# A depthwise convolution shared by four engines: 22 of 31 taps of two channel tiles as ScalarE products and GpSimd adds

## The chip, the cores and the metric

One core of a Trainium2 chip runs the kernel. The time is device microseconds of one execution, lower is better; the median of the runs is compared. The engines are TensorE (PE; PEld is its weight load), VectorE (DVE), ScalarE (ACT), GpSimd (POOL) and SyncE (SP), which issues the DMAs of the weights here.

## The reference, cut to what matters

Two layers of a transformer on 2 x 128 tokens (128 context tokens and 128 latents), width 1024: first attention with a short convolution and a dense SwiGLU, then a Conformer convolution and a mixture of 8 experts. The change lies in the Conformer convolution, a depthwise convolution of 31 taps over the tokens of each of the two sequences, of 1024 channels:

```python
def _conformer_conv(h, p):
    z = h @ p["w_pw1"] + p["b_pw1"]
    a, g = jnp.split(z, 2, axis=-1)
    u = a * jax.nn.sigmoid(g)
    u = lax.conv_general_dilated(
        u, p["w_dw"][:, None, :], window_strides=(1,),
        padding=((CONF_KERNEL // 2, CONF_KERNEL // 2),),
        dimension_numbers=('NWC', 'WIO', 'NWC'),
        feature_group_count=u.shape[-1]) + p["b_dw"]
    u = jax.nn.silu(_layernorm(u, p["ln_g"], p["ln_b"]))
    return u @ p["w_pw2"] + p["b_pw2"]
```

Everything is float32.

## The kernel before

Activations stand transposed, channels on the partitions: hid, xT and uT have 8 tiles (KT) of 128 channels by 256 tokens (two blocks of 128; uT has 15 columns of zeros on both sides of each block). Weights come in pieces of 1 MB into a ring of 7 slots (raw), in the order of ORDER; ACT rounds each into high, DVE subtracts (low), and PE multiplies in three passes. The ada pieces, the conditioning, are used by PE straight from raw (ada_piece).

Each engine has its own hand-written program; they meet at semaphores. In the convolution stage the order is this. PE computes pw1 in four units of two channel tiles; ACT makes the sigmoid (glu_gate), DVE the product into uT (glu, line 1230). As soon as tiles 0 and 1 are there, DVE begins their taps between its low parts, and it goes on with tiles 2, 3 and 4 in turn: one scalar_tensor_tensor a tap, hid = uT shifted x tap + hid (conv_taps, lines 1236 to 1248; the first tap adds the bias). It waits each time for its own tap of the same tile before. Between them stand rows_out(4), which copies PE's sums of the conditioning out of PSUM into ada4 (line 934), and mod_out(4) (line 945), which adds a bias to them. Tiles 5, 6 and 7 (DVE_TILES = 5 and up) are multiplied by PE: ACT scales the identity by the 128 taps of a tile (diag, line 714, a ring of DIAGS = 6), and PE multiplies uT by it and accumulates in PSUM (line 1835). ACT takes each finished tile out with its bias (conv_out, line 700). PE does ada_sum(4) after the first of its tiles, and one ada_piece of group 5 after each further 6 taps. ada_sum(4) waits for rows_out(4), and the first piece of group 5 for mod_out(4).

When all eight tiles are done, PE adds them over the channels with a matrix of ones (ln_sums, line 1842), DVE subtracts the mean (line 1276), ACT squares (line 722), PE sums again (line 1537), POOL takes the root, and pw2 follows, then the routing and the experts. The sums wait for DVE's tiles by conv_part and for PE's by conv_pe_ready.

POOL has little to do: the roots (line 437), the DMAs of the gate's bias, pw2_gb (line 455, waits for ada_out), and the bias added to xT (line 458, 128x2048).

## Time and profile before

| | us |
|---|---|
| Median of 3 runs | 1578.24 (1577.27 to 1578.58) |
| The profiled execution | 1578.13, of which span 1576.3 |
| PE busy | 1504.0 (95%) |
| PE weight loads busy | 1263.9 (80%) |
| DVE busy | 1194.9 (76%) |
| ACT busy | 969.1 (61%) |
| POOL busy | 22.7 (1%) |

The page gives one execution, taken by the hardware profiler. Engine times are the union of their instructions; PE's ends are modelled, and matmuls overlap. A float32 matmul stands as two records of each kind, so 93 taps are 186 records. In a timeline a row merges instructions of one line: its first number is the start of the first, its second the time to the end of the last. Instructions of DVE and ACT overlap a little, so that the distance between two is less than one's duration.

### The profile page before, as it was taken

How to read it: one execution, taken by the hardware profiler on the slowest of the kernel's cores; microseconds unless marked ns; L12 is line 12 of the kernel's file. 1: busy time of each engine (PE TensorE's matmuls, PEld its weight loads, DVE VectorE, ACT ScalarE, POOL GpSimd, SP SyncE). 2: the span in 40 equal slices, each digit the busy share in tenths (PEclk: the TensorE clock that was granted, in tenths of full speed). 3: DMA queues.
4: the chain of work that ended last, by engine and by line, in shares of the span. 5: the costliest groups of instructions: out<-in, count | busy, mean ns of one | idle time of the engine just before them, and what ended most of it. 6: DMA issues, size and time to landing. Idle time of an engine off the chain costs nothing.

```text
span 1576.3 us, 22550 instructions
## 1 busy us (share of the span) xinstructions
PE 1504.0 (95%) x8346; PEld 1263.9 (80%) x8346; DVE 1194.9 (76%) x1195; ACT 969.1 (61%) x989; POOL 22.7 (1%) x28
## 2 busy tenths in 40 slices
PE   5979989999999879999999999999999999999997
PEld 2858789998887768888888888888888888888885
DVE  2547564444798568889879889888988997988996
ACT  2436253432547357777776777777777777776773
POOL 0110000000000000000000000000000000000000
PEclk9989999999999879999999999999999999999999
DMA  9654586665744429989989998998998998998993
GB/s 364 253 218 176 176 299 222 226 202 192 263 161 161 161 84 373 374 338 355 372 340 357 374 363 330 371 378 323 370 374 323 372 373 323 370 375 322 372 374 132
DMA packets 100877, 468.56 MB, mean 297 GB/s; under 512 B 8108, under 2 KB 38972, under 8 KB 51664
## 3 DMA queue, kind: packets, MB, share of 16 engines
q1 hardware_dynamic: 99408, 464.81, 78.4%
q10 hardware_dynamic: 864, 1.76, 0.3%
q0 software_dynamic: 544, 1.15, 0.2%
q8 instruction: 41, 0.67, 0.2%
q14 instruction: 20, 0.16, 0.0%
HBM read 466.55 MB, written 1.14 MB: 297 GB/s over the span
## 4 chain that ended last, share of the span: by engine, by line
PE 90%; DVE 4%; DMA 2%; ACT 2%; issue 1%; POOL 0%; SPq 0%; ACTq 0%; DVEq 0%
PE bank L1507 20%; PE bank L1505 20%; PE bank L1506 20%; PE bank L1511 6%; PE bank L1512 5%; PE bank L1513 5%; PE bank L1522 2%; PE bank L1935 2%; DMA raw<-ada_w 2%; PE bank L1835 2%; PE bank L1963 2%; PE bank L1790 1%; PE bank L1791 1%; PE bank L1792 1%; DVE hid L1248 1%; PE bank L1537 1%
## 5 line engine op out<-in xcount | busy, mean ns | idle before, releaser
L1401 DVE TENSOR_TENSOR low<-raw,high 128x2048 fp32r<-128x2048 f32 x333 | 748.5, 2289 | 118.3 <-ACT high L784 113.6
L784 ACT ACTIVATE high<-raw 128x2048 fp32r<-128x2048 f32 x333 | 626.6, 1920 | 75.3 <-DMA raw<-moe 70.6
L1505 PE MATMUL bank<-high,hidH 128*128 128x512 f32 x896 | 350.9, 392 | 3.1 <-ACT hidL L774 3.1
L1507 PE MATMUL bank<-high,hidL 128*128 128x512 f32 x896 | 349.9, 391 | 0.0
L1506 PE MATMUL bank<-low,hidH 128*128 128x512 f32 x896 | 349.5, 390 | 0.0
L1511 PE MATMUL bank<-hidH,high 128*128 128x256 f32 x736 | 213.4, 290 | 16.3 <-DVE hidL L912 5.1
L1512 PE MATMUL bank<-hidL,high 128*128 128x256 f32 x736 | 210.9, 287 | 0.0
L1513 PE MATMUL bank<-hidH,low 128*128 128x256 f32 x736 | 210.7, 286 | 0.0
L1505 PEld LDWEIGHTS bank<-high,hidH 128*128 128x128 f32 x896 | 168.7, 188 | 38.0 <-ACT hidL L774 3.5
L1507 PEld LDWEIGHTS bank<-high,hidL 128*128 128x128 f32 x896 | 168.6, 188 | 35.2
L1506 PEld LDWEIGHTS bank<-low,hidH 128*128 128x128 f32 x896 | 168.7, 188 | 34.7
L1505 PE MATMUL bank<-high,upH 128*128 128x512 f32 (+1 forms) x462 | 189.8, 411 | 2.4 <-DVE low L858 2.4
L858 DVE TENSOR_TENSOR low<-raw,high 128x2048 fp32r<-128x2048 f32 (+2 forms) x59 | 132.8, 2262 | 74.4 <-ACT high L490 74.2
L1507 PE MATMUL bank<-high,upL 128*128 128x512 f32 (+1 forms) x462 | 181.9, 394 | 0.0
L1506 PE MATMUL bank<-low,upH 128*128 128x512 f32 (+1 forms) x462 | 181.3, 393 | 0.0
L1511 PEld LDWEIGHTS bank<-hidH,high 128*128 128x128 f32 x736 | 144.1, 196 | 28.4 <-issue 17.3
L490 ACT ACTIVATE high<-raw 128x2048 fp32r<-128x2048 f32 (+2 forms) x59 | 110.8, 1887 | 73.0 <-DMA raw<-ffn_gu 48.2
L788 ACT ACTIVATE eact<-bank 128x256 f32<-128x256 f32 x112 | 43.2, 386 | 170.4 <-PE bank L1507 170.4
L1512 PEld LDWEIGHTS bank<-hidL,high 128*128 128x128 f32 x736 | 144.1, 196 | 0.0
L1513 PEld LDWEIGHTS bank<-hidH,low 128*128 128x128 f32 x736 | 144.0, 196 | 0.0
L1507 PEld LDWEIGHTS bank<-high,upL 128*128 128x128 f32 x462 | 87.4, 189 | 18.4
L1505 PEld LDWEIGHTS bank<-high,upH 128*128 128x128 f32 x462 | 87.6, 190 | 17.7 <-issue 3.2
(225 smaller groups left out, 1381.2 us busy)
## 6 DMA issues: line engine op xcount, KB each, us to landing
raw<-moe SPq DMA_DIRECT2D x336, 1024.0 KB, 4.8
raw<-ada_w SPq DMA_DIRECT2D x48, 1024.0 KB, 6.1
raw<-ffn_gu SPq DMA_DIRECT2D x44, 512.0 KB, 5.0
raw<-ffn_down SPq DMA_DIRECT2D x11, 1024.0 KB, 7.1
raw<-w_in SPq DMA_DIRECT2D x8, 1024.0 KB, 10.2
raw<-conv_pw SPq DMA_DIRECT2D x16, 512.0 KB, 5.2
raw<-w_o SPq DMA_DIRECT2D x4, 1024.0 KB, 6.2
raw<-conv_pw SPq DMA_DIRECT2D x4, 1024.0 KB, 5.3
```

Source lines behind the costliest of these rows:

```text
L490: a.activation(high[:, n % SPLITS, 0:w], raw[:, m % RAWS, 0:w], ACT.Copy).then_inc(S("high_ready"), 1)
L784: a.activation(high[:, m % SPLITS, :], raw[:, n % RAWS, :], ACT.Copy).then_inc(S("high_ready"), 1)
L788: a.activation(eact[:, u % 2, :], bank[:, u % 2, 0:UNIT], ACT.Silu).then_inc(S("e_silu"), 1)
L858: v.tensor_tensor(low[:, STREAM[SPLIT[n]] % RAWS, 0:w], raw[:, STREAM[SPLIT[n]] % RAWS, 0:w], high[:, n % SPLITS, 0:w].bitcast(F32), ALU.s ...
L1401: v.tensor_tensor(low[:, n % RAWS, :], raw[:, n % RAWS, :], high[:, m % SPLITS, :].bitcast(F32), ALU.subtract).then_inc(S("low_ready"), 1)
L1505: pe.matmul(out, xh, wh, start=start, stop=False)
L1506: pe.matmul(out, xh, wl, start=False, stop=False)
L1507: return pe.matmul(out, xl, wh, start=False, stop=stop)
L1511: pe.matmul(out, wh, hidH[:, kk, :], start=start, stop=False)
L1512: pe.matmul(out, wh, hidL[:, kk, :], start=False, stop=False)
L1513: return pe.matmul(out, wl, hidH[:, kk, :], start=False, stop=stop)
L1522: last = pe.matmul(bank[32 * c:32 * c + 32, 6, :], cond[:, k, :], raw[:, m % RAWS, c * 512:(c + 1) * 512], start=k == 0, stop=k == KT - 1)
```

## The change

- The taps are divided anew. DVE does tiles 0 to 3 whole and taps 0 to 8 of tile 4. PE does taps 0 to 8 of tile 5 and tiles 6 and 7 whole (PE_TAPS, 71). Taps 9 to 30 of tiles 4 and 5 (PRODUCTS, 44) are multiplied by ACT, each into a slot of prod (a ring of PRODS = 4), the first two straight into pool_part.
- POOL adds each further product to pool_part, its half for the tile, 42 adds of 128x256. From the third add on it waits for its own add two before.
- DVE joins: hid[4] += pool_part[0], and hid[5] = PE's part from bank 2 + bias + pool_part[1]. The sums of the layernorm wait for this.
- The ring of diagonals has 12 slots instead of 6. ACT makes 12 ahead of glu_gate(2) and 12 products ahead of glu_gate(3), then two diagonals and a product in turn.
- rows_out(4) stands after 5 taps of tiles 2 to 4 instead of 8, mod_out(4) after 9 instead of 11. PE does ada_sum(4) after 30 of its taps, and the pieces of group 5 after 36, 42 and so on.
- POOL does its adds before pw2_gb and the bias of xT.

```diff
--- before.py
+++ after.py
@@ -41,7 +41,8 @@
 Z0 = Q_LORA + KV_LORA + ROPE
 RAWS = 7
 SPLITS = 6
-DIAGS = 6
+DIAGS = 12
+PRODS = 4
 PIECE = 2048
 GROUP = 2048
 GC = GROUP // 512
@@ -64,7 +65,11 @@
 NPAR = _c
 
 
-DVE_TILES = 5
+DVE_TILES = 4
+SHARED = 9
+POOL_TILES = (4, 5)
+PRODUCTS = [(k, j) for j in range(SHARED, TAPS) for k in POOL_TILES]
+PE_TAPS = [(5, j) for j in range(SHARED)] + [(k, j) for k in (6, 7) for j in range(TAPS)]
 PHASE = 12480
 NORM_C, LAT_C, HEAD_C = 8, 10, 16
 HSS_C = HEAD_C + 5 * HEADS
@@ -213,6 +218,8 @@
         sg = sb("sg", [P, UC, TILES, P], where=ph)
         sq = sb("sq", [P, KT, TOK], where=ph)
         diag = sb("diag", [P, DIAGS, P], where=ph)
+        prod = sb("prod", [P, PRODS, TOK], where=ph)
+        pool_part = sb("pool_part", [P, len(POOL_TILES), TOK], where=ph)
         ph.close()
         sb("phase_space", [P, PHASE])
         const = sb("const", [P, C_END])
@@ -450,6 +457,13 @@
                 src = t["ada_b"][1:2, 5 * D + half * 512:5 * D + (half + 1) * 512]
                 for tt in range(TILES):
                     pool.dma_start(gate_b[p0 + tt:p0 + tt + 1, :], src).then_inc(S("gate_bias"), 16)
+            for i in range(2, len(PRODUCTS)):
+                half = PRODUCTS[i][0] - POOL_TILES[0]
+                pool.wait_ge(S("product_ready"), i + 1)
+                if i >= 4:
+                    pool.wait_ge(S("product_added"), i - 3)
+                st.mark(pool.tensor_tensor(pool_part[:, half, :], pool_part[:, half, :], prod[:, i % PRODS, :], ALU.add),
+                        "product_added")
             b0 = COLS["pw2_b"][0]
             pool.wait_ge(S("ada_out"), 10)
             st.do(pool.tensor_tensor(pw2_gb[:, :, :], mod[:, 1, 2], par[:, b0:b0 + KT].unsqueeze(2).to_broadcast(
@@ -695,28 +709,52 @@
                                          ACT.Sigmoid, bias=par[:, b:b + 1]), "sg_ready")
 
             def conv_out(k):
-                a.wait_ge(S("tap_used"), (k - DVE_TILES + 1) * TAPS)
+                a.wait_ge(S("tap_used"), PE_TAPS.index((k, TAPS - 1)) + 1)
                 b = COLS["dw_b"][0] + k
                 st.mark(a.activation(hid[:, k, :], bank[:, 4 + k % 2, 0:TOK], ACT.Identity,
                                      bias=par[:, b:b + 1]), "conv_pe_ready")
+
+            def diagonals(i0, i1):
+
+                for i in range(i0, min(i1, len(PE_TAPS))):
+                    k, j = PE_TAPS[i]
+                    if i >= DIAGS:
+                        a.wait_ge(S("tap_used"), i - DIAGS + 1)
+                    st.mark(a.activation(diag[:, i % DIAGS, :], ident, ACT.Copy,
+                                         scale=taps[:, j * KT + k:j * KT + k + 1]), "diag_ready")
+
+            def products(i0, i1):
+
+                if i0 == 0:
+                    a.wait_ge(S("state_out"), 32)
+                for i in range(i0, min(i1, len(PRODUCTS))):
+                    k, j = PRODUCTS[i]
+                    a.wait_ge(S("glu_ready"), k + 1)
+                    half = k - POOL_TILES[0]
+                    if i >= PRODS + 2:
+                        a.wait_ge(S("product_added"), i - PRODS - 1)
+                    dst = pool_part[:, half, :] if i < 2 else prod[:, i % PRODS, :]
+                    st.mark(a.activation(dst.rearrange("p (t n) -> p t n", t=TILES), uT[:, k, :, j:j + P], ACT.Copy,
+                                         scale=taps[:, j * KT + k:j * KT + k + 1]), "product_ready")
 
             for u in range(4):
                 if u < 3:
                     named("pw1", "a", u + 1)
                     named("pw1", "b", u + 1)
+                if u == 2:
+                    diagonals(0, DIAGS)
+                if u == 3:
+                    products(0, 12)
                 glu_gate(u)
 
-            for k in range(DVE_TILES, KT):
-                for j in range(TAPS):
-                    i = (k - DVE_TILES) * TAPS + j
-                    if i >= DIAGS:
-                        a.wait_ge(S("tap_used"), i - DIAGS + 1)
-                    st.mark(a.activation(diag[:, i % DIAGS, :], ident, ACT.Copy,
-                                         scale=taps[:, j * KT + k:j * KT + k + 1]), "diag_ready")
-                if k > DVE_TILES:
-                    conv_out(k - 1)
-                    named("pw2", 0, k - DVE_TILES - 1)
-            conv_out(KT - 1)
+            for n in range(len(PRODUCTS) - 12):
+                diagonals(DIAGS + 2 * n, DIAGS + 2 * n + 2)
+                products(12 + n, 13 + n)
+                if n == 16:
+                    named("pw2", 0, 0)
+            conv_out(6)
+            named("pw2", 0, 1)
+            conv_out(7)
             for k in range(KT):
                 a.wait_ge(S("centred"), k + 1)
                 st.mark(a.activation(sq[:, k, :], hid[:, k, :], ACT.Square), "ln_sq")
@@ -1261,14 +1299,21 @@
             conv_taps((0, 1), 16, 26)
             glu(3)
             conv_taps((0, 1), 26, TAPS)
-            rest = tuple(range(2, DVE_TILES))
-            conv_taps(rest, 0, 8)
+            conv_taps((2, 3, 4), 0, 5)
             rows_out(4)
-            conv_taps(rest, 8, 11)
+            conv_taps((2, 3, 4), 5, SHARED)
             mod_out(4)
-            conv_taps(rest, 11, 25)
+            conv_taps((2, 3), SHARED, 23)
             named("pw2", 0, 0)
-            conv_taps(rest, 25, TAPS)
+            conv_taps((2, 3), 23, TAPS)
+            v.wait_ge(S("conv_part"), st.n["conv_part"])
+            v.wait_ge(S("product_added"), len(PRODUCTS) - 3)
+            st.mark(v.tensor_tensor(hid[:, 4, :], hid[:, 4, :], pool_part[:, 0, :], ALU.add), "conv_part")
+            v.wait_ge(S("product_added"), len(PRODUCTS) - 2)
+            v.wait_ge(S("tap_used"), SHARED)
+            b = COLS["dw_b"][0] + 5
+            st.mark(v.scalar_tensor_tensor(hid[:, 5, :], bank[:, 2, 0:TOK], par[:, b:b + 1], pool_part[:, 1, :], ALU.add,
+                                           ALU.add), "conv_part")
             named("pw2", 0, 1)
 
             v.wait_ge(S("ln_sum"), 1)
@@ -1823,17 +1868,16 @@
                 if u:
                     ada_piece(4, 4 + u)
 
-            def conv_taps(k, j0, j1):
-
-                if j0 == 0:
-                    pe.wait_ge(S("glu_ready"), k + 1)
-                    if k >= DVE_TILES + 2:
-                        pe.wait_ge(S("conv_pe_ready"), k - DVE_TILES - 1)
-                for j in range(j0, j1):
-                    i = (k - DVE_TILES) * TAPS + j
+            def conv_taps(i0, i1):
+
+                for i in range(i0, i1):
+                    k, j = PE_TAPS[i]
+                    if i == 0 or PE_TAPS[i - 1][0] != k:
+                        pe.wait_ge(S("glu_ready"), k + 1)
                     pe.wait_ge(S("diag_ready"), i + 1)
-                    st.mark(pe.matmul(bank[:, 4 + k % 2, 0:TOK].rearrange("p (t n) -> p t n", t=TILES),
-                                      diag[:, i % DIAGS, :], uT[:, k, :, j:j + P], start=j == 0, stop=j == TAPS - 1),
+                    last = SHARED - 1 if k == 5 else TAPS - 1
+                    st.mark(pe.matmul(bank[:, 2 if k == 5 else 4 + k % 2, 0:TOK].rearrange("p (t n) -> p t n", t=TILES),
+                                      diag[:, i % DIAGS, :], uT[:, k, :, j:j + P], start=j == 0, stop=j == last),
                             "tap_used")
 
             def ln_sums(ks, first, last):
@@ -1843,17 +1887,16 @@
                                     stop=last and k == ks[-1])
                 return ins
 
-            cuts = [(k, j) for k in range(DVE_TILES, KT) for j in range(0, TAPS, 6)]
-            for i, (k, j) in enumerate(cuts):
-                conv_taps(k, j, min(j + 6, TAPS))
-                if i == 5:
+            for n, i in enumerate(range(0, len(PE_TAPS), 6)):
+                conv_taps(i, min(i + 6, len(PE_TAPS)))
+                if n == 4:
                     ada_sum(4)
-                if i >= 6 and i < 12:
-                    ada_piece(5, i - 6)
-            pe.wait_ge(S("conv_part"), DVE_TILES * TAPS)
-            ln_sums(tuple(range(DVE_TILES)), True, False)
-            pe.wait_ge(S("conv_pe_ready"), KT - DVE_TILES)
-            st.mark(ln_sums(tuple(range(DVE_TILES, KT)), False, True), "ln_sum")
+                if n >= 5 and n < 11:
+                    ada_piece(5, n - 5)
+            pe.wait_ge(S("conv_part"), DVE_TILES * TAPS + SHARED + 2)
+            ln_sums(tuple(range(6)), True, False)
+            pe.wait_ge(S("conv_pe_ready"), 2)
+            st.mark(ln_sums((6, 7), False, True), "ln_sum")
             ada_piece(5, 6)
             ada_piece(5, 7)
             for k in range(KT):
```

## Rows read from the trace of the kernel before

**Rows 1.** The page: shares of the chain that ended last, and a group of VectorE.

```profile
PE 90%; DVE 4%; DMA 2%; ACT 2%; issue 1%; POOL 0%; SPq 0%; ACTq 0%; DVEq 0%
...
L1401 DVE TENSOR_TENSOR low<-raw,high 128x2048 fp32r<-128x2048 f32 x333 | 748.5, 2289 | 118.3 <-ACT high L784 113.6
```

**Rows 2.** Busy us (and instructions) of each engine by windows: convolution, experts.

```profile
core 0: us, PE busy (x) PEld busy (x) DVE busy (x) ACT busy (x) POOL busy (x), PEclk, DMA share, GB/s
...
453.00:503.00 50.00, 48.79 (x243) 36.53 (x244) 47.81 (x109) 39.53 (x97) 4.22 (x2) 1.00 0.47 167
...
590.00:1560.00 970.00, 970.00 (x4501) 803.15 (x4500) 850.90 (x635) 707.80 (x609) 0.00 (x0) 1.00 0.92 354
```

**Rows 3.** Timeline, start and end of the convolution: start us, us, engine, line, operation, count.

```profile
453.17 7.16 PE L1835 MATMUL bank<-uT,diag 128*128 128x256 f32 x32 [0.31 <-ACT diag L714]
...
488.41 1.06 PE L1522 MATMUL bank<-raw,cond 128*32 128x512 f32 x8
...
489.40 13.68 PE L1835 MATMUL bank<-uT,diag 128*128 128x256 f32 x62
...
493.70 7.21 DVE L1248 SCALAR_TENSOR_TENSOR hid<-uT,par,hid 128x256 f32<-128x256 f32 x18
...
502.92 3.62 PE L1842 MATMUL bank<-hid,const 128*128 128x256 f32 x16
```

**Rows 4.** Timeline of ScalarE: sigmoids, a weight piece, unhindered diagonals, squares.

```profile
426.50 0.84 ACT L694 ACTIVATE sg<-bank,par 128x256 f32<-128x256 f32 x2 [3.07 <-PE bank L1513]
...
485.39 1.90 ACT L490 ACTIVATE high<-raw 128x2048 fp32r<-128x2048 f32 x1
487.19 1.85 ACT L714 ACTIVATE diag<-const,par 128x128 f32<-128x128 f32 x6
...
507.04 2.73 ACT L722 ACTIVATE sq<-hid 128x256 f32<-128x256 f32 x8 [3.44 <-DVE hid L1276]
```

**Rows 5.** Timeline of GpSimd, 471 to 477 us.

```profile
471.56 0.51 POOL L455 TENSOR_TENSOR pw_gb<-mod,par 128x16 f32<-128x16 f32 x1 [70.93 <-DVE mod L945]
472.15 3.71 POOL L458 TENSOR_TENSOR xT<-xT,pw_gb 128x2048 f32<-128x2048 f32 x1
```

**Rows 6.** VectorE's taps: the tile uT (ns min/median/max), then its timeline.

```profile
engine op xcount: duration ns min/median/max, first and last start us, forms
...
L1248 DVE SCALAR_TENSOR_TENSOR hid<-uT,par,hid x150: 475/480/3834, 421.4 to 500.4; 128x256 f32<-128x256 f32 x150
...
471.51 0.88 DVE L1248 SCALAR_TENSOR_TENSOR hid<-uT,par,hid 128x256 f32<-128x256 f32 x2
...
471.92 4.23 DVE L1248 SCALAR_TENSOR_TENSOR hid<-uT,par,hid 128x256 f32<-128x256 f32 x2
...
476.07 2.06 DVE L1248 SCALAR_TENSOR_TENSOR hid<-uT,par,hid 128x256 f32<-128x256 f32 x5
```

**Rows 7.** Timeline of VectorE ahead of the last GLU gate.

```profile
441.75 8.01 DVE L1248 SCALAR_TENSOR_TENSOR hid<-uT,par,hid 128x256 f32<-128x256 f32 x20
452.77 0.88 DVE L1230 SCALAR_TENSOR_TENSOR uT<-bank,par,sg 128x256 f32<-128x256 f32 x2 [3.01 <-ACT sg L694]
```

**Rows 8.** Granted clock by windows, and TensorE's thin matmuls by timeline.

```profile
562.00:566.00 4.00, 2.09 (x18) 1.85 (x18) 2.54 (x10) 1.85 (x2) 0.00 (x0) 0.99 0.00 0
566.00:570.00 4.00, 2.88 (x14) 2.91 (x14) 3.59 (x4) 0.96 (x3) 0.00 (x0) 0.50 0.02 4
...
503.00:510.00 7.00, 7.00 (x48) 4.87 (x47) 5.04 (x9) 3.53 (x11) 0.00 (x0) 1.00 0.00 0
512.00:518.00 6.00, 3.32 (x13) 2.95 (x13) 3.85 (x9) 2.74 (x6) 0.71 (x1) 0.50 0.00 0
...
508.32 4.27 PE L1537 MATMUL bank<-const,sq 128*128 128x2 f32 x32
...
545.02 3.13 PE L1537 MATMUL bank<-const,hid 128*128 128x2 f32 x16 [1.98 <-ACT hid L501]
```


## Prediction

> **What bounds the kernel now.** The page comes first: the chain that ended last is TensorE for 90% of the span [rows 1]. The stages follow from the busy table by windows. From 590 us to the end, the stage of the experts, PE is busy for all of its 970 us at full clock [rows 2]: whatever reaches that stage late or early moves the end by as much. DMA share is 0.92 there, but it starts its loads on the releases of the same chain, so it moves along. The stage that changes is the convolution, 453 to 503 us, where PE, DVE and ACT are busy 48.8, 47.8 and 39.5 of 50 us and POOL 4.2 [rows 2]. The timelines show what ends it. DVE starts its last 18 taps at 493.70 and is done at 500.91; PE's last 31 taps end at 503.08, and its sums of the tiles for the layernorm (L1842) start at 502.92 [rows 3]. So PE ends the stage now, and DVE is only 2.0 us behind the point at which it would. Taking taps off both at once is a sensible aim; the question is what GpSimd does to DVE.
>
> **The change part by part.** The code has 8 x 31 = 248 taps. Before, DVE does 155 and PE 93. After, DVE does 4 x 31 + 9 = 133, PE 9 + 62 = 71, and 44 are products on ACT: two go straight into the partial sums, 42 are adds on POOL.
>
> PE: 62 records are 31 taps in 13.68 us [rows 3], (13.68 - 0.38)/31 = 0.43 us a tap. 22 fewer are 9.5 us less.
>
> DVE: 18 taps take 7.21 us [rows 3]; with one duration of 0.48 taken off, the other 17 follow at 0.396 us. 22 fewer are 8.7 us less. The two joins cost one pitch each, 0.8 us more.
>
> ACT: it makes 22 diagonals fewer and 44 products more. Diagonals that need not wait for PE come 6 in 1.85 us [rows 4], 0.29 us apart. A product of 128x256 has no row; the squares, 8 in 2.73 us, give 0.33 and the sigmoids, 2 in 0.84, give 0.37 [rows 4]. The product reads two strided halves of SBUF and scales by a column; I take 0.36. An iteration of the new loop (two diagonals, one product) is then 2 x 0.29 + 0.36 = 0.94 us against 0.86 for PE's two taps, and PE has six pieces of the conditioning between (1.0 us each [rows 3]). 32 iterations and one weight piece (1.90 [rows 4]) are 32 us, within the 50 of the stage, so ACT is hidden. If that cover went, each 0.1 us on a product would cost at most 3.2 us.
>
> POOL: an add of 128x256 has no row. The two ordinary TENSOR_TENSORs of this engine in the trace took 0.51 us for 16 elements a partition and 3.71 for 2048 [rows 5]: 1.57 ns an element over 0.49 us, so 0.89 us by my estimate for 256. 42 of them are 37 us, and ACT delivers a product only each 0.95 to 1.3 us. POOL has that time.
>
> But POOL does not run beside DVE for nothing. While POOL adds the bias to xT (472.15 to 475.86), one DVE tap takes 3.83 us against a median of 0.48. It is the second of the two that start at 471.92 and end 4.23 us later, so it starts at 472.31, and the next starts at 476.07 [rows 5, 6]. That is 476.07 - 472.31 - 0.40 = 3.36 us lost in a POOL instruction of 3.71: all but 0.35 us. Such a tap reads uT and hid, both in SBUF, and POOL's add reads two tensors in SBUF, as the 42 new ones do. The small POOL operation just before (0.51 us) cost DVE nothing that shows: two taps in 0.88 us, the ordinary pace [rows 5, 6]. So the price of one add to DVE lies between 0.89 - 0.51 = 0.38 us (all that the small one hides stays hidden) and 0.89 (nothing is). I take 0.89 - 0.35 = 0.54, from the large one, which is the only row in which the price can be seen. The break-even is much lower, since 42 adds pay for only 22 taps.
>
> The Trainium skill speaks against this change. Its page "SBUF — State Buffer", section "Who interferes with whom", says that a VectorE instruction with two SBUF inputs and a GpSimd instruction that reads SBUF exclude one another for the whole instruction, whichever starts second waiting. The trace agrees in kind; in size the rule would make the price the whole 0.89 instead of 0.54, and the sum below 14.7 us more. "GPSIMD Engine Reference", section "Instruction dispatch", puts a two-input loop at about 2.5 cycles an element, an estimate of 0.53 us for 256 elements where the slope of the rows gives 0.40; 42 times the difference would be 5.5 us more. The operand of the large row was a broadcast, so no run here shows which holds.
>
> The sum, along DVE. The first 12 products come before the last gate of the GLU; ten of them are added beside DVE's taps 16 to 25 of tiles 0 and 1, which start at 441.75 and take 8.01 us; DVE then waits 3.01 us for the sigmoid until 452.77 [rows 7]. With ten adds at 0.54 these taps end at 441.75 + 8.01 + 5.4 = 455.2 instead, and the last tap's end overlaps the next instruction by 0.1: DVE is 2.3 us late there. The other 32 adds fall into the stretch up to the joins: 32 x 0.54 = 17.3. The 3.36 us of the xT add were paid before and are paid again: POOL comes to it after its adds, which I put at about 500 us, and DVE still has taps then. End of DVE's part: 500.9 + 2.3 - 8.7 + 17.3 + 0.8 = 512.6, so the layernorm's sums start 9.8 us later than 502.92 did (0.1 for the semaphore).
>
> What is late next. PE now waits for DVE inside the convolution too: its ada_sum(4) stands after 30 taps (its taps begin at 453.2 [rows 3] and 30 x 0.43 is 12.9, so about 466 us) and needs rows_out(4), which is behind 25 of DVE's taps, and its next piece needs mod_out(4), 12 taps later. By the same prices these come at about 474 (from 456.1, 25 taps are 9.9 us and some 15 adds 8.1) and 482 (the copy 0.6, 12 taps 4.8, four adds 2.2). Behind PE stand ACT's diagonals (a ring of 12) and so its products. PE has then 35 taps and 6 pieces left, 15 + 6 = 21 us, and ends at 503 to 507, before DVE; this costs nothing by itself. But PE is then idle for some us ahead of the sums. In this trace the granted clock goes from 1.00 to 0.50 of full, 2.4 to 1.2 GHz, after a few thinly used us: PE is busy for 2.1 of the 4 us from 562, and the next window is at 0.50; it is also at 1.00 from 503 to 510 but at 0.50 from 512 to 518, after the thin matmuls (L1537) [rows 8]. The 16 records of the sums run at full clock now, 502.92 to 506.54 [rows 3], some 3.4 us from the first to behind the last. At half clock they take 3.4 us more. The 32 records of L1537 behind them take 4.27 us now, and 16 of them took 3.13 at a low clock [rows 8]; that would be 2.0 more, and 0.7 for the conditioning pieces. I take the 3.4 and leave the 2.7 to the range. Nothing later changes, and the low clock that now begins at about 511 would only begin earlier.
>
> Sum: 9.8 + 3.4 = 13.2 us on the profiled run's own 1578.13 us (span 1576.3), which is 0.1 below the median of the three runs: 1591.3 us. Its own range: at 0.38 an add 42 x 0.16 = 6.7 less and no clock effect, 1581.2; at 0.89 and the full clock effect 14.7 + 2.7 more, 1608.7.
>
> **The rivals.** First, faster: short POOL operations slip between the taps as the 0.51 us one did. In favour is that row, against it that 256 elements at 1.57 ns are 0.40 us of data, more than is free between two taps: DVE's large subtract takes 2289 ns for 2048 elements [rows 1], so a tap's 256 are some 0.29 of its pitch of 0.40. Then DVE ends at 500.9 - 8.7 + 0.8 = 493.0, PE at 503.1 - 9.5 = 493.6, and the sums start 9.3 us earlier: 1568.8 us. It decides below 0.2 us an add, where 32 adds are under 6.4 us. Chance 0.13.
>
> Second, a small price, 0.2 to 0.3 us an add: 32 x 0.3 = 9.6, DVE ends at 502.6 without the late gate, and PE's end is about the same. No change, 1575 to 1581 us. Chance 0.10.
>
> Third, VectorE's queue of taps keeps POOL out, and POOL becomes the bound: if each add waits for two taps, it is 0.89 + 0.8 = 1.7 us, and the chain of 42 from 442.5 on ends at 514; with the clock that is 1578.1 + 11.2 + 3.4 = 1592.7, and 1.9 more where the xT add and DVE's low part of the second pw2 weight then collide. Against it: POOL's xT add got in ahead of a DVE tap that started 0.16 us after it [rows 5, 6]. Chance 0.12. That leaves 0.65 for the forecast.
>
> **How the numbers follow.** Forecast 1591.3. The range leaves out most of the faster rival and the top of the price: 1577 to 1607. Some 0.2%, 3.2 us, is about what a measurement of this kernel can tell from no change. Slower by more: 0.65 + 0.12 = 0.77; within: 0.10; faster: 0.13. That the change does not do what it says is no case of its own: the counts of taps follow from the lists.
>
> **What would show each step.** In the changed profile DVE's taps (the scalar_tensor_tensor of uT) should have many durations near 1.0 to 1.4 us instead of 0.48, and their total time should exceed 128 x 0.40 by some 20 us. POOL's 42 adds should last 0.9 to 1.3 us each. ACT's products should stand 0.36 us apart where nothing holds them. PE should wait for the copy to ada4 after 30 taps, and again ahead of the sums, with 0.50 in the clock column there. The sums should start near 512.7 and the experts' stage be as long as now. The prediction is wrong if the taps keep their 0.48 beside the adds; it has the wrong culprit if DVE's join waits for product_added, or if PE's last tap comes after the joins.

## The result

The changed kernel takes 1589.65 us (median of 5 runs, 1585.1 to 1590.82), the kernel before 1578.24 (median of 5, 1576.9 to 1578.99). The ratio is 1.0065, 95% interval 1.0047 to 1.0083: slower by 0.65%. The profiled execution took 1589.98 us with a span of 1588.1, 11.8 more than before's 1576.3.

VectorE's timeline from the last but one gate of the GLU to the layernorm (start us, us, engine, line, operation, tiles, shapes, count; where a bracket stands, the idle time before and what ended it):

```profile
444.75 12.86 DVE L1286 SCALAR_TENSOR_TENSOR hid<-uT,par,hid 128x256 f32<-128x256 f32 x20
457.54 0.86 DVE L1268 SCALAR_TENSOR_TENSOR uT<-bank,par,sg 128x256 f32<-128x256 f32 x2
458.44 7.88 DVE L1286 SCALAR_TENSOR_TENSOR hid<-uT,par,hid 128x256 f32<-128x256 f32 x10
...
474.73 0.68 DVE L972 COPY ada<-bank 128x512 f32<-128x512 f32 x1
475.33 4.83 DVE L1286 SCALAR_TENSOR_TENSOR hid<-uT,par,hid 128x256 f32<-128x256 f32 x12
...
480.48 18.19 DVE L1286 SCALAR_TENSOR_TENSOR hid<-uT,par,hid 128x256 f32<-128x256 f32 x28
...
511.95 0.48 DVE L1315 SCALAR_TENSOR_TENSOR hid<-bank,par,pool_part 128x256 f32<-128x256 f32 x1
```

The 20 taps ahead of the last gate take 12.86 us instead of 8.01 [rows 7]; the 10 behind it 7.88 (before: 4.05). Where no add is made, from 475.33 on, 12 taps take 4.83 us, the old pace. The joins end at 512.43.

The taps and the adds by tile (ns min/median/max, then first and last start in us). The longest tap is again the one beside the bias of xT:

```profile
L1286 DVE SCALAR_TENSOR_TENSOR hid<-uT,par,hid x128: 470/474/3826, 424.0 to 511.1; 128x256 f32<-128x256 f32 x128
...
L465 POOL TENSOR_TENSOR pool_part<-pool_part,prod x42: 723/904/2772, 445.8 to 499.2; 128x256 f32<-128x256 f32 x42
```

TensorE's timeline. It waits for the copy to ada4 after 30 taps (475.46) and for the joins after its last tap (512.48), where before it was its own last tap that ended the stage [rows 3]:

```profile
455.32 13.25 PE L1879 MATMUL bank<-uT,diag 128*128 128x256 f32 x60
475.46 1.87 PE L1575 MATMUL bank<-const,ada 128*128 128x8 f32 x8 [6.90 <-DVE ada L972]
...
501.33 2.43 PE L1879 MATMUL bank<-uT,diag 128*128 128x256 f32 x10
512.48 6.25 PE L1886 MATMUL bank<-hid,const 128*128 128x256 f32 x16 [8.72 <-DVE hid L1315]
...
520.52 3.73 PE L1582 MATMUL bank<-const,sq 128*128 128x2 f32 x32
```

Granted clock (the first number behind POOL's count) in that gap and behind it:

```profile
508.00:512.00 4.00, 0.00 (x0) 0.00 (x0) 3.97 (x12) 0.00 (x0) 0.00 (x0) 0.50 0.00 0
512.00:516.00 4.00, 3.52 (x8) 2.86 (x9) 2.62 (x3) 0.00 (x0) 0.00 (x0) 0.50 0.02 4
...
520.00:524.00 4.00, 4.00 (x39) 3.48 (x32) 1.51 (x5) 3.98 (x8) 0.00 (x0) 1.00 0.00 0
```

PE does nothing from 503.8 to 512.5 and the clock is at 0.50 from 508 to 516; the 16 records of the sums take 6.25 us instead of 3.62 [rows 3]. The thin matmuls behind them take 3.73 instead of 4.27 [rows 8]: here the clock is back at 1.00 by 520, while in the kernel before it fell during them (0.92 from 508 to 512, 0.50 behind).

The stage of the experts is as long as before; a window of 970 us looks like that in [rows 2]:

```profile
600.00:1570.00 970.00, 970.00 (x4499) 803.25 (x4498) 850.86 (x634) 708.63 (x609) 0.00 (x0) 1.00 0.92 355
```

**Where the 11.8 us are.** The stages can be set against each other from one mark, the start of the last two sigmoids on ScalarE. In before's timeline it is

```profile
451.90 0.84 ACT L694 ACTIVATE sg<-bank,par 128x256 f32<-128x256 f32 x2 [11.86 <-PE bank L1513]
```

and in after's

```profile
454.43 0.84 ACT L708 ACTIVATE sg<-bank,par 128x256 f32<-128x256 f32 x2 [2.78 <-PE bank L1558]
```

From there to the sums of the layernorm: 51.0 us before, 58.1 after, 7.0 more. From the sums to the end: 1073.4 and 1075.6, 2.2 more. The remaining 2.5 us lie ahead of the mark. The sigmoids wait for PE there, and up to the mark PE has the same work as before and waits for none of the new instructions (ACT's first diagonals and products and ten of the adds do run in that stretch). In that stretch the clock was granted differently, between 390 and 410 us of after

```profile
390.00:410.00 20.00, 16.86 (x98) 9.51 (x97) 11.86 (x36) 8.56 (x20) 2.65 (x5) 0.74 0.63 211
```

and of before

```profile
390.00:410.00 20.00, 16.64 (x111) 10.97 (x108) 12.22 (x37) 10.12 (x21) 2.65 (x5) 0.83 0.63 211
```

(0.74 against 0.83 of full clock; from 180 to 220 us it is 0.83 against 0.91). The profiles of the experiments below, variants of either kernel, put the mark at 450.8 to 456.0 (453.3 to 455.5 in variants of the kernel before), so a difference of 2.5 us there needs no change to explain it.

The division is a reading of one profile of each kernel, and these scatter too. Two profiles of one and the same kernel (a_psum and a_psum_again below) are 3.0 us apart from the mark to the sums, and from the sums to the end the twelve profiles of the experiments took 1071.8 to 1076.0 us. In what follows each profile is read from its own mark.

### The profile page after: what moved, and what is told of

It reads as the page before. It is cut to its first block, busy times and chain, and to the rows that moved or that the text cites. A ratio compares the mean times of both kernels' runs of the same rounds, so it can differ in the third digit from the quotient of the medians.

```text
span 1588.1 us, 22586 instructions
## 1 busy us (share of the span) xinstructions
PE 1504.2 (95%) x8302; PEld 1262.6 (80%) x8302; DVE 1205.6 (76%) x1175; ACT 973.5 (61%) x1010; POOL 60.3 (4%) x70
## 4 chain that ended last, share of the span: by engine, by line
PE 86%; DVE 7%; DMA 3%; ACT 2%; issue 1%; SPq 0%; POOL 0%; ACTq 0%; DVEq 0%
PE bank L1550 20%; PE bank L1552 20%; PE bank L1551 20%; PE bank L1556 5%; PE bank L1557 5%; PE bank L1558 5%; DVE hid L1286 4%; PE bank L1978 2%; PE bank L1567 2%; DMA raw<-ada_w 2%; PE bank L2006 2%; PE bank L1836 1%; PE bank L1835 1%; PE bank L1837 1%; DMA raw<-conv_pw 1%
```

## The experiments

Each ratio is to the kernel before, run beside it on the same chip; the medians of the kernel before were 1579.9 us (beside the b_ runs), 1580.2 (a_set, a_psum, a_warm, a_half) and 1579.8 (a_psum_all, a_psum_again). The two runs at the end are one execution each, beside 1580.55. Theory A: GpSimd's adds, which read SBUF, hold up VectorE's taps, which read two tensors in SBUF. Theory B: the loss comes from the new waits between engines and their order.

**Twenty adds, beside the kernel before (b_add20).**

```diff
+            pool.wait_ge(S("conv_part"), 68)
+            st.do(pool.memset(spare[:, :, :], 0.0), "spare_set")
+            for i in range(20):
+                if i >= 2:
+                    pool.wait_ge(S("spare_done"), i - 1)
+                st.mark(pool.tensor_tensor(spare[:, i % 2, :], spare[:, i % 2, :], spare[:, 2 + i % 2, :], ALU.add), "spare_done")
             b0 = COLS["pw2_b"][0]
             pool.wait_ge(S("ada_out"), 10)
```

> The kernel before, with 20 GpSimd adds of 128x256 on spare tiles (two SBUF inputs each) put beside VectorE's taps, after tiles 0 and 1 are done; nothing uses them. Theory A (a GpSimd instruction that reads SBUF holds up VectorE's two-input taps): in the changed kernel 10 adds cost the taps 4.85 us, 0.48 each, so 20 cost 9 to 10 us; VectorE had 2.0 us to spare at the end of the stage, so the layernorm's sums start 7 to 8 us later, and with a low clock there the kernel takes 1585 to 1589 us. Theory B (the changed kernel lost its time to its new waits between engines, not to the adds as such): these adds wait for nobody and nobody waits for them, so 1578 us as before, and taps of 0.48 us throughout.

Measured: 1587.25 us, ratio 1.0048 (1.0034 to 1.0062). From the mark to the sums 57.6 us, 6.6 more than before. VectorE's rows, and the adds:

```profile
470.35 0.69 DVE L941 COPY ada<-bank 128x512 f32<-128x512 f32 x1
470.95 7.41 DVE L1255 SCALAR_TENSOR_TENSOR hid<-uT,par,hid 128x256 f32<-128x256 f32 x9
...
478.69 24.84 DVE L1255 SCALAR_TENSOR_TENSOR hid<-uT,par,hid 128x256 f32<-128x256 f32 x42
...
464.41 23.20 POOL L459 TENSOR_TENSOR spare<-spare 128x256 f32<-128x256 f32 x20
...
L459 POOL TENSOR_TENSOR spare<-spare x20: 899/904/6612, 464.4 to 486.7; 128x256 f32<-128x256 f32 x20
```

The stretches of 9 and 42 taps took 3.65 and 20.07 us before; together they lose 8.5 us to 20 adds, 0.43 each, a little less than the 9 to 10 us expected. Nobody waits for these adds, so theory B has nothing to say here. The loss reaches the sums by two ways: VectorE's last tap ends at 512.85, and PE, which waited 3.94 us for the later mod_out(4), starts its sums right behind its own last tap at 512.91. One thing was not expected: the first add took 6.6 us, and VectorE's taps beside it kept their pace. Its end falls on VectorE's copy of ada4.

**Twenty copies, twenty memsets (b_copy20, b_set20).** The same place, another instruction:

```diff
-                st.mark(pool.tensor_tensor(spare[:, i % 2, :], spare[:, i % 2, :], spare[:, 2 + i % 2, :], ALU.add), "spare_done")
+                st.mark(pool.tensor_copy(spare[:, i % 2, :], spare[:, 2 + i % 2, :]), "spare_done")   # b_copy20
+                st.mark(pool.memset(spare[:, i % 2, :], 0.0), "spare_done")                           # b_set20
```

> The same with 20 GpSimd copies of 128x256 in place of the adds, one SBUF input each. Theory A with the loss set by the time in which GpSimd reads: some half of the adds' loss, 4 to 5 us on VectorE, 1580 to 1584 us. If only two-input instructions of GpSimd hold up VectorE: no loss, 1578 us.

Measured: 1581.55 us, ratio 1.0016 (1.0006 to 1.0026).

```profile
469.91 4.75 DVE L1255 SCALAR_TENSOR_TENSOR hid<-uT,par,hid 128x256 f32<-128x256 f32 x9
...
474.99 21.24 DVE L1255 SCALAR_TENSOR_TENSOR hid<-uT,par,hid 128x256 f32<-128x256 f32 x42
...
L459 POOL COPY spare<-spare x20: 391/587/6307, 463.3 to 478.9; 128x256 f32<-128x256 f32 x20
```

The two stretches lose 1.1 + 1.2 = 2.3 us, 0.11 a copy: a quarter of what an add costs, less than the half that was expected. The first copy, too, took long: 6.3 us, again to the copy of ada4. The taps beside the others take 0.61 us instead of 0.48.

> The same with 20 GpSimd memsets of 128x256, which read nothing. Theory A (it is the reading that collides): taps keep 0.48 us, 1578 us. If any GpSimd instruction that touches SBUF holds up VectorE: a loss of 0.3 to 0.5 us each, 1582 to 1587 us.

Measured: 1580.51 us, ratio 1.0001 (0.9989 to 1.0012).

```profile
469.22 3.65 DVE L1255 SCALAR_TENSOR_TENSOR hid<-uT,par,hid 128x256 f32<-128x256 f32 x9
...
473.21 20.13 DVE L1255 SCALAR_TENSOR_TENSOR hid<-uT,par,hid 128x256 f32<-128x256 f32 x42
...
L459 POOL MEMSET spare<- x20: 311/312/313, 462.7 to 467.5; 128x256 f32 x20
```

The taps have the times of before. It is GpSimd's reading of SBUF that costs VectorE, and two inputs cost more than twice as much as one. (Why more than twice: below, at the length of an add.)

**VectorE's partial sums in PSUM, kernel before (b_psum).**

```diff
+PART_BANK = {2: 0, 3: 1, 4: 3}
...
-                        dst = hid4[:, k, :, :]
+                        old = hid4[:, k, :, :]
+                        if k in PART_BANK:
+                            old = bank[:, PART_BANK[k], 0:TOK].rearrange("p (t n) -> p t n", t=TILES)
+                        dst = hid4[:, k, :, :] if j == TAPS - 1 else old
...
-                            st.mark(v.scalar_tensor_tensor(dst, src, w, dst, ALU.mult, ALU.add), "conv_part")
+                            st.mark(v.scalar_tensor_tensor(dst, src, w, old, ALU.mult, ALU.add), "conv_part")
```

> The kernel before with VectorE's partial sums of tiles 2, 3 and 4 kept in PSUM (banks 0, 1 and 3) instead of SBUF, so that a tap reads one tensor in SBUF. GpSimd has only the bias of xT there. Theory A: the tap of 3.83 us during that instruction is gone (0.48 to 0.55 us), VectorE's part ends 3 to 4 us earlier; PE ended the stage by 2 us anyway, so the kernel takes 1576 to 1579 us. If the taps are held for another reason than two inputs from SBUF, the long tap stays. If PSUM makes a tap slower by 0.05 us, 93 taps cost 4.6 us and the gain is eaten.

Measured: 1579.84 us, ratio 1.0007 (0.9996 to 1.0019).

```profile
473.86 16.55 DVE L1252 SCALAR_TENSOR_TENSOR bank<-uT,par,bank 128x256 f32<-128x256 f32 x42
...
473.91 0.21 POOL L456 TENSOR_TENSOR pw_gb<-mod,par 128x16 f32<-128x16 f32 x1 [71.31 <-DVE mod L946]
474.21 3.61 POOL L459 TENSOR_TENSOR xT<-xT,pw_gb 128x2048 f32<-128x2048 f32 x1
...
L1252 DVE SCALAR_TENSOR_TENSOR bank<-uT,par,bank x87: 479/485/489, 461.1 to 498.0; 128x256 f32<-128x256 f32 x87
```

With one input from SBUF no tap is held beside the bias of xT: 42 taps in 16.55 us instead of 20.07, at most 489 ns each. PE ends the stage, so nothing is won. And GpSimd's small operation now takes 0.21 us where it took 0.51 [rows 5]: that one had waited for a tap.

**The changed kernel with memsets for adds (a_set).** The products are not added, so a part of the convolution is left out.

```diff
-                st.mark(pool.tensor_tensor(pool_part[:, half, :], pool_part[:, half, :], prod[:, i % PRODS, :], ALU.add),
+                st.mark(pool.memset(prod[:, i % PRODS, :], 0.0),
                         "product_added")
```

> The changed kernel with each of its 42 GpSimd adds replaced by a memset of the same 128x256 (the products are not added, so that part of the convolution is left out); every wait and mark stays. The memset cost VectorE nothing where it was tried. Theory A (the adds' reads are the loss): the last gate is no longer late (2.3 us), 32 adds no longer cost 0.43 to 0.48 us each; VectorE still pays 3.4 us for the bias of xT. VectorE's part ends some 16 us earlier than in the changed kernel, PE's some 9 to 10; sums of the layernorm 9 us earlier than in the kernel before, 1569 to 1573 us. Theory B (the loss is in the new waits and the order): 1586 to 1590 us as the changed kernel.

Measured: 1569.97 us, ratio 0.9939 (0.9922 to 0.9955). The mark and the sums:

```profile
455.28 0.84 ACT L708 ACTIVATE sg<-bank,par 128x256 f32<-128x256 f32 x2 [4.99 <-PE bank L1558]
...
495.05 3.62 PE L1886 MATMUL bank<-hid,const 128*128 128x256 f32 x16
```

From the mark to the sums 39.8 us, against 58.1 in the changed kernel: all waits and the order are the same, and 18.3 us are gone. Theory B falls. One step of the expectation failed: the bias of xT no longer held a tap for 3.4 us. It came at 492.44, behind the taps, and held VectorE's low part there (5.30 us instead of 2.28), ahead of which the joins were done; so its 3.4 us are part of what went, beside the adds.

**The changed kernel with partial sums in PSUM (a_psum, a_psum_all).** a_psum is the edit of b_psum in the changed kernel, with the join of tile 4 reading bank 3. a_psum_all adds tiles 0 and 1:

```diff
-PART_BANK = {2: 0, 3: 1, 4: 3}
+PART_BANK = {0: 7, 1: 5, 2: 0, 3: 1, 4: 3}
...
                     if i == 0 or PE_TAPS[i - 1][0] != k:
                         pe.wait_ge(S("glu_ready"), k + 1)
+                    if (k, j) == (7, 0):
+                        pe.wait_ge(S("conv_part"), 2 * TAPS)
```

> The changed kernel with VectorE's partial sums of tiles 2, 3 and 4 in PSUM (banks 0, 1, 3), so that its taps read one tensor in SBUF; GpSimd's adds as they are. Theory A: only the taps of tiles 0 and 1 are still held up (10 adds before the last gate, some 5 after it), the rest keep 0.48 us; VectorE ends at about 497 us of a profile whose earlier stages run as in the profile of after, PE at 499 and so PE ends the stage; the sums start at about 499.5 instead of 512.5, at full clock: 1572 to 1576 us, faster than both kernels. Theory B: as the changed kernel. The kernel before with the same edit took 1579.8 us, no different from before, so the edit by itself gives nothing.

Measured: 1573.68 us, ratio 0.9967 (0.9953 to 0.9981), faster than both kernels; 45.5 us from the mark to the sums. The 66 taps that keep their sums in PSUM are free of the adds beside them, the 60 of tiles 0 and 1 are not (17 of them take 0.94 us or more):

```profile
L1290 DVE SCALAR_TENSOR_TENSOR bank<-uT,par,bank x66: 472/484/490, 463.7 to 492.3; 128x256 f32<-128x256 f32 x66
L1290 DVE SCALAR_TENSOR_TENSOR hid<-uT,par,hid x60: 472/480/1002, 420.7 to 461.9; 128x256 f32<-128x256 f32 x60
```

The same kernel ran again beside a_psum_all:

> The kernel of a_psum again, beside the one above and on the same chip, to compare the two: 1572 to 1575 us, some 3 to 4 us over a_psum_all.

Measured: 1576.66 us, ratio 0.9977 (0.9965 to 0.9988), above the 1572 to 1575 expected. From the mark to the sums 48.5 us, 3.0 more than in the profile above: VectorE's copy of ada4 came 1.6 us later from the mark, and PE waited 5.4 us for it. No tap with its sum in PSUM is over 0.49 us here either.

> As a_psum, and the partial sums of tiles 0 and 1 in PSUM too (banks 7 and 5; PE's tile 7, which uses bank 5, waits for them). Theory A: the taps of tiles 0 and 1 also keep 0.48 us beside the adds (10 and 5 of them now cost 4.9 and 3.4 us), the last gate is not late, and PE no longer waits 3.8 us for the copy to ada4. From PE's first tap to the sums 39 us as with the memsets, instead of 43.0 with a_psum: 1568 to 1571 us. If something else than the second input from SBUF is left, the 20 taps ahead of the last gate still take 12.9 us and the time is that of a_psum.

Measured: 1570.61 us, ratio 0.9934 (0.9915 to 0.9954).

```profile
L1290 DVE SCALAR_TENSOR_TENSOR bank<-uT,par,bank x124: 470/480/490, 425.8 to 491.7; 128x256 f32<-128x256 f32 x124
...
L466 POOL TENSOR_TENSOR pool_part<-pool_part,prod x42: 720/730/2929, 447.1 to 491.4; 128x256 f32<-128x256 f32 x42
...
495.80 3.62 PE L1892 MATMUL bank<-hid,const 128*128 128x256 f32 x16
```

No tap is over 0.49 us, an add takes 0.73 instead of 0.90, and from the mark (456.03) to the sums it is 39.8 us, the same as with the memsets. So the adds, which are made here and waited for, cost nothing any more, and PE ends the stage. By the medians the kernel takes 9 us less than the kernel before beside it, 6 less than a_psum_again (3 to 4 were expected), and 19 less than the changed kernel, which was measured at another time.

**Half of the products (a_half).** SHARED = 20 instead of 9, the loops lengthened to match, mod_out(4) left after 9 taps.

> The changed kernel with 11 products of each of the two tiles instead of 22 (taps 20 to 30): VectorE takes 11 taps more (144), PE 11 more (82), GpSimd makes 20 adds. Theory A: VectorE pays 11 x 0.40 = 4.4 us for taps and saves 22 x 0.45 = 9.9 us of stalls, so its part ends 5 to 6 us earlier than in the changed kernel; PE's last tap 4.7 us later, at about 508; sums start at 507 to 509: 1583 to 1587 us. Theory B: the sums wait on PE and ACT, about 1590 us.

Measured: 1580.88 us, ratio 1.0005 (0.9996 to 1.0015), no different from before, and below the 1583 to 1587 expected.

```profile
477.58 18.93 DVE L1286 SCALAR_TENSOR_TENSOR hid<-uT,par,hid 128x256 f32<-128x256 f32 x39
...
505.43 0.48 DVE L1316 SCALAR_TENSOR_TENSOR hid<-bank,par,pool_part 128x256 f32<-128x256 f32 x1
...
499.53 7.19 PE L1880 MATMUL bank<-uT,diag 128*128 128x256 f32 x32
506.56 3.62 PE L1887 MATMUL bank<-hid,const 128*128 128x256 f32 x16
```

The joins end at 505.9, by the marks 5.9 us earlier than in the changed kernel, as expected from fewer adds; PE's last tap ends at 506.7, and PE ends the stage again, 52.7 us from the mark. Since PE is not idle ahead of the sums, these also have the full clock again (3.62 us), which is 2.6 us of what the changed kernel lost.

**PE kept at work ahead of the sums (a_warm).**

```diff
+            pe.wait_ge(S("conv_pe_ready"), 2)
+            for _ in range(18):
+                pe.matmul(bank[:, 3, 0:TOK], ones, uT[:, 7, 0, 0:P].unsqueeze(1).to_broadcast([P, TILES, P]), start=True, stop=True)
             pe.wait_ge(S("conv_part"), DVE_TILES * TAPS + SHARED + 2)
```

> The changed kernel with 18 matmuls of 128x256 that nothing uses on PE between its last tap and the sums of the layernorm, where PE was idle for 8.7 us and the granted clock fell to 0.50. If the clock is a term of its own, the 16 records of the sums take 3.6 instead of 6.2 us, and the kernel is 2 to 4 us faster than the changed one, 1585 to 1587 us; the start of the sums does not move. If the clock falls for another reason, no change, 1589 us.

Measured: 1587.83 us, ratio 1.0058 (1.0041 to 1.0075), not apart from the changed kernel's 1.0065. The trace shows why:

```profile
502.39 8.04 PE L1898 MATMUL bank<-uT,const 128*128 128x256 f32 x36 [0.56 <-ACT hid L714]
510.27 3.62 PE L1886 MATMUL bank<-hid,const 128*128 128x256 f32 x16
...
502.00:510.00 8.00, 7.61 (x35) 6.73 (x36) 7.97 (x13) 0.34 (x1) 2.29 (x1) 1.00 0.21 88
510.00:514.00 4.00, 4.00 (x22) 3.22 (x25) 1.27 (x2) 0.00 (x0) 0.00 (x0) 1.00 0.00 0
```

The clock stays at 1.00 and the sums take 3.62 us instead of 6.25, so the clock is a cost of PE's idle time. But the 18 matmuls hold PE beyond the end of the joins (508.99): the sums start 1.3 us behind it, 59.5 us from the mark instead of 58.1; half of the 2.6 us is spent again. The 2 to 4 us that were expected did not show in the time. That a shorter filling would win the rest was not tried.

**When the first add gets in (b_add20_apart, b_add20_late).** The memset moved ahead; in the second the adds wait for conv_part 113, inside the row of 42 taps. One execution each, so their times are worth less than their traces.

> As b_add20, where the first of the 20 adds took 6.6 us beside taps of the usual 0.48 us and came in only at VectorE's copy of ada4; from there on adds and taps took turns, 0.87 us a pair. Here the memset of the spare tiles is moved some 30 taps ahead, so that the first add comes from rest. If it was the memset right before it that let it wait, the first add takes 0.7 to 1.1 us and the turns start at once: 20 adds in 18 us. If VectorE's unbroken queue of taps keeps GpSimd out, the first add again takes some us, to the copy of ada4 at the latest.

Measured: 1588.68 us; the first add again took long, 7.6 us, to the copy of ada4. So the memset in front of it had no part in it.

> As b_add20_apart, with the adds starting in the long row of 42 taps after mod_out(4). If the unbroken queue keeps GpSimd out, the first add lasts up to the low part of pw2 (10 us and more), the adds run mostly behind it, and the sums start 2 to 4 us later instead of 6.6. If not, they take turns at once: 20 adds, 9 us on VectorE, sums 7 us later than in the kernel before.

Measured: 1582.54 us. From the mark to the sums 54.2 us, 3.2 more than before instead of 6.6.

```profile
472.85 16.71 DVE L1256 SCALAR_TENSOR_TENSOR hid<-uT,par,hid 128x256 f32<-128x256 f32 x42
489.48 2.28 DVE L866 TENSOR_TENSOR low<-raw,high 128x2048 fp32r<-128x2048 f32 x1
491.68 15.70 DVE L1256 SCALAR_TENSOR_TENSOR hid<-uT,par,hid 128x256 f32<-128x256 f32 x18
...
480.22 12.13 POOL L460 TENSOR_TENSOR spare<-spare 128x256 f32<-128x256 f32 x1 [32.86 <-DVE hid L1256]
```

The first add lasts 12.13 us, while the 42 taps take 16.71, undisturbed. It gets in behind VectorE's low part, which begins at 489.48, takes 2.28 us and reads two tensors in SBUF as well; from there on 18 taps take 15.70 us instead of 7.21, one add a tap. In this kernel an unbroken row of two-input taps keeps GpSimd out altogether, and once it is in, the two take turns. A fixed cost of the first add would not fit: it would not be 6.6, 7.6 and 12.1 us, each time up to another instruction of VectorE. The same shows once in the order of the changed kernel: in a_set, GpSimd's small operation came behind eleven undisturbed taps, ran 2.37 us where it takes 0.21 alone, and ended as the row of taps did.

## Why the prediction was right, point by point

The forecast was 1591.3 us, 13.2 over the profiled run; measured were 11.8 in the profiles and 11.4 in the medians. The direction and its cause were right; of the size, 9.2 us belong to the change by the marks (7.0 + 2.2), where 13.2 were forecast, and 2.5 came from the granted clock in earlier stages, of which no step spoke: that part of the agreement is luck. How much of the 11.4 in the medians is of that kind is not shown; 9.2 lies in their interval, which is 7.4 to 13.1 us.

- **The price of an add, 0.54 us.** Too high by 0.08. From the rows of the changed kernel against those of a_set and before: 4.85 us for the 10 adds ahead of the gate, 14.6 for the other 32, so 19.4 / 42 = 0.46. The forecast had 22.7 in all. The 32 adds, 17.3 forecast, are the difference between 9.8 and 7.0 us at the sums. How the price is made up is plainer than the interpolation: each add holds one tap, which takes 0.95 us instead of 0.48 (38 of the 128 taps took 0.67 us or more beside the one of 3.83; the rest of the adds fell on the first taps of tiles 2 to 4 and the low part).
- **The length of an add, 0.89 us.** The median is 0.904, but for another reason than the one given. Unhindered it takes 0.73 (a_psum_all); the row of 0.51 us that gave the intercept had a wait for a tap in it. The bounds 0.38 and 0.89 held. That 0.89 - 0.35 = 0.54 came so near is in part luck, since both were too large. With the unhindered lengths one rule fits all three prices: an instruction of GpSimd holds a tap for its length less 0.26 us. The add: 0.73, and the tap takes 0.47 more; the bias of xT: 3.61 (b_psum), and 3.35 more; the copy: 0.39, and 0.13 more. That is also why a copy costs less than half of an add. With this rule the forecast's step would have given 0.47. (By 0.21 us for 16 elements, one operand a broadcast, and 0.73 for 256, an element of an add costs 2.15 ns, an estimate; the prediction had 1.57.)
- **"VectorE is 2.3 us late at the gate."** The gate starts 3.1 us after the mark, before 0.9: 2.2.
- **VectorE's end, 512.6.** 512.43, of which 2.5 are the earlier stages; by the marks 509.9. The close agreement is luck: a price too high by as much as the earlier stages, unforeseen, were longer.
- **The bias of xT still inside the taps.** It ran at 502.44, beside a tap of 3.83 us, as said.
- **PE late at ada_sum(4) and at the sums, ends before DVE.** It waited 6.9 us for the copy, which ended at 475.4 (472.9 by the mark; forecast 474), and its last tap ended at 503.8. It cost nothing by itself, though the clock fell there too (0.50 from 474 to 478).
- **ACT hidden.** Its products are 0.40 us apart instead of 0.36, an iteration 0.98 instead of 0.94:

```profile
445.24 2.10 ACT L737 ACTIVATE prod<-uT,par 128x256 f32<-128x256 f32 x5
...
456.80 0.49 ACT L737 ACTIVATE prod<-uT,par 128x256 f32<-128x256 f32 x1
...
457.78 0.50 ACT L737 ACTIVATE prod<-uT,par 128x256 f32<-128x256 f32 x1
```

- **The clock, 3.4 us.** The sums lost 2.6, since the clock rose before they were done (0.79 of full on the mean from 516 to 520), where the forecast had all 16 records at 0.50; half a us came back in the thin matmuls. That makes 2.1, and from the sums to the end it was 2.2 more, but this stretch scatters by more than that, so the rows are the evidence and not the sum.
- **The rivals.** Short operations that slip between the taps: fell; the 42 adds cost 19.4 us. A small price: fell. GpSimd kept out by the queue of taps: not in the changed kernel, where the longest add, 2.77 us, stood behind the low part; but the mechanism is real, as b_add20_late shows, and the evidence given against it, that the xT add got in ahead of a tap, was poor: that add came 0.7 us behind mod_out(4), a break in the queue, with GpSimd's small operation between. Its time, 1592.7, came from two taps an add; in the runs it is either one a tap or none.
- **What the profile should show.** Taps of 1.0 to 1.4 us were forecast, they are 0.95; "some 20 us" more in total is 19.4. The adds were to last 0.9 to 1.3 us; 19 of the 42 lasted less than 0.9, down to 0.72. Waits and clock column as said.

Of the Trainium skill, "SBUF — State Buffer", section "Who interferes with whom", the runs bear out that a VectorE instruction with two SBUF inputs contends with a GpSimd instruction that reads SBUF (a tap 0.95 us instead of 0.48, an add 0.90 instead of 0.73), and that one which only writes SBUF does not take part (b_set20: taps as before). They bear out that a tap with one SBUF input, the other in PSUM, is free (at most 0.49 us). Not every VectorE instruction with one tensor in SBUF is: two of the first taps of tiles 2 to 4, a TENSOR_SCALAR that reads uT alone, took 0.87 and 0.82 us beside adds, where the third took 0.40; the section has its rule only for instructions outside what it calls the 2-port perf modes, and no run here shows in which mode these ran.

```profile
L1283 DVE TENSOR_SCALAR hid<-uT,par x5: 404/415/872, 423.3 to 467.4; 128x256 f32<-128x256 f32 x5
```

The section calls the lock exclusive; taken as the prediction took it, the second waiting for the whole instruction, it did not give the size. The loss is 0.46 us for an add of 0.90 beside taps and 0.73 alone, and with the whole 0.89 the forecast would have been 14.7 us higher.

Open is why the adds of the changed kernel got in at once while those of b_add20 waited for a break. The number of undisturbed taps ahead does not settle it: an add of the changed kernel got in without a wait behind four (at 484.29), the first one of b_add20_apart was kept out behind four. Nor does the order of the tiles, since a_set, with the changed kernel's order, shows such a wait too. The traces do not show what lets GpSimd in.

## What to carry to other kernels

Ahead of moving elementwise work to GpSimd, look at how many SBUF inputs VectorE's instructions beside it have. One long VectorE row next to a GpSimd row is enough to estimate the price (here 0.54 for 0.46), if the GpSimd length is not itself taken from a row with a wait in it; and the price per instruction times their number stands against the work saved (here 42 x 0.46 against 22 x 0.40). If VectorE accumulates, keep the accumulator in PSUM: here the tap cost the same, and GpSimd's work became free. A wait of PE can cost twice, the wait and the low clock behind it, as the 8.7 us ahead of the sums did here (in b_add20_late a wait of 3.0 us there did not: its sums took 3.72 us).

## What the runs showed of the hardware that was not expected

- A copy on GpSimd (one SBUF input) costs VectorE's taps 0.11 us, an add (two) 0.43 to 0.46, a memset nothing, all of 128x256 float32. For the copy, the add and the large bias of xT it is the unhindered length less 0.26 us that one tap is held.
- An unbroken row of two-input taps on VectorE kept a GpSimd add waiting for 12.13 us; it got in behind the low part there, at the copy of ada4 in b_add20, b_add20_apart and (a copy on GpSimd) b_copy20, and then one add went with one tap, 0.87 us a pair.
- scalar_tensor_tensor with its accumulator in PSUM, read and written, has the same pace as in SBUF: 20 taps in 7.93 us against 8.01 [rows 7], and 480 ns at the median in both.
